# Seven-product gate tiles: the rest of a pair behind the next tile's first copy, the fourth weight sum ahead of the row scaling, an own place for the second gate tile

## The reference, cut to what matters

```python
def swiglu(h, wg, wu, wd):            # h 512x1024, wg and wu 1024x2816, wd 2816x1024
    return (jax.nn.silu(h @ wg) * (h @ wu)) @ wd

for i in range(2):
    x = x + 0.5 * swiglu(rmsnorm_2(x, ffn_norm1[i]), ffn1_wg[i], ffn1_wu[i], ffn1_wd[i])
    # ... attention ...
    x = x + 0.5 * swiglu(rmsnorm_2(x, ffn_norm2[i]), ffn2_wg[i], ffn2_wu[i], ffn2_wd[i])
```

## Time and profile before

| | |
|---|---|
| median of 3 runs | 2733.34 us (2733.22 to 2733.67) |
| profiled execution | 2736.7 us, its span 2735.5 us |
| PE busy | 2645.6 us, 97% of the span |
| DVE, ACT, POOL busy | 1572.2, 1084.5, 598.2 us |
| mean granted clock of TensorE | 0.987 |

### The profile page before, as it was taken

One profiled execution on the slowest core, in us unless ns is written; L12 is line 12 of the kernel. 1 busy time (PEld: TensorE's weight loads), 2 busy tenths in 40 slices (PEclk: granted clock), 3 DMA queues, 4 the chain that ended last, 5 costly groups with the idle time before them and its releaser, 6 DMA issues.

```text
span 2735.5 us, 33395 instructions
## 1 busy us (share of the span) xinstructions
PE 2645.6 (97%) x13532; PEld 2254.5 (82%) x13532; DVE 1572.2 (57%) x2410; ACT 1084.5 (40%) x1797; POOL 598.2 (22%) x574
## 2 busy tenths in 40 slices
PE   9999999999999999999989999999999999899998
PEld 8888888888887887889878888788888888788887
DVE  7538457574766444457774545664545685654543
ACT  4344234242553222257642323442324685432322
POOL 0000010000120000036521312323222685322220
PEclk9999999999999999999999999999999999999999
DMA  5322325323323444364223232232322101232322
GB/s 157 124 93 80 106 95 186 131 78 109 106 77 108 108 90 108 81 121 118 79 70 107 78 108 93 77 116 81 108 81 92 36 32 47 77 108 69 117 62 78
DMA packets 276401, 259.07 MB, mean 95 GB/s; under 512 B 40324, under 2 KB 266647, under 8 KB 276247
## 3 DMA queue, kind: packets, MB, share of 16 engines
q1 hardware_dynamic: 276231, 256.93, 31.2%
q10 hardware_dynamic: 16, 0.00, 0.0%
HBM read 242.23 MB, written 14.68 MB: 94 GB/s over the span
## 4 chain that ended last, share of the span: by engine, by line
PE 70%; issue 9%; DVE 7%; POOL 7%; ACT 4%; DMA 3%; POOLq 0%; SPq 0%; ACTq 0%; DVEq 0%
PE bank L1464 21%; PE bank L1466 21%; PE bank L1465 21%; DMA RAW<-in_ffn_wg 3%; PE bank L1564 1%; PE bank L1565 1%; PE bank L1566 1%; POOL M L2887 1%; POOL TMP L2908 1%; POOL M L2885 1%; POOL RAW L2895 1%; DVE Wl L2267 1%; POOL RAW L2888 1%; PE bank L1651 1%; DVE bank L2374 1%
## 5 line engine op out<-in xcount | busy, mean ns | idle before, releaser
L1464 PE MATMUL bank<-Hh,Wl 128*128 128x512 f32 x1704 | 674.7, 396 | 17.7 <-DVE Wl L2267 16.9
L1465 PE MATMUL bank<-Hl,Wh 128*128 128x512 f32 x1704 | 667.0, 391 | 0.0
L1466 PE MATMUL bank<-Hh,Wh 128*128 128x512 f32 x1704 | 666.5, 391 | 0.0
L2267 DVE TENSOR_TENSOR Wl<-RAW,Wh 128x1024 fp32r<-128x1024 f32 (+1 forms) x366 | 473.1, 1335 | 138.2 <-ACT Wh L1864 137.6
L1864 ACT ACTIVATE Wh<-RAW 128x1024 fp32r<-128x1024 f32 (+2 forms) x400 | 387.3, 1019 | 271.1 <-PE bank L1466 213.9
L1464 PE MATMUL bank<-Ph,Wl 128*128 128x512 f32 x1152 | 451.9, 392 | 0.8 <-DVE Wl L2267 0.4
L1466 PE MATMUL bank<-Ph,Wh 128*128 128x512 f32 x1152 | 448.6, 389 | 0.0
L1465 PE MATMUL bank<-Pl,Wh 128*128 128x512 f32 x1152 | 448.1, 389 | 0.0
L1464 PEld LDWEIGHTS bank<-Hh,Wl 128*128 128x128 f32 x1704 | 322.2, 189 | 87.8 <-DVE Wl L2267 19.2
L1466 PEld LDWEIGHTS bank<-Hh,Wh 128*128 128x128 f32 x1704 | 321.7, 189 | 68.5
L1465 PEld LDWEIGHTS bank<-Hl,Wh 128*128 128x128 f32 x1704 | 322.3, 189 | 65.7 <-issue 1.7
(11 more groups left out here) (385 smaller groups left out, 4073.8 us busy)
## 6 DMA issues: line engine op xcount, KB each, us to landing
RAW<-in_ffn_wg SPq DMA_DIRECT2D x44, 1024.0 KB, 5.3
RAW<-in_ffn_wu SPq DMA_DIRECT2D x44, 1024.0 KB, 5.4
RAW<-in_ffn_wd SPq DMA_DIRECT2D x32, 1024.0 KB, 4.9
RAW<-in_w_up SPq DMA_DIRECT2D x22, 1024.0 KB, 5.1
RAW<-in_w_in SPq DMA_DIRECT2D x20, 1024.0 KB, 5.2
RAW<-in_ffn_wd SPq DMA_DIRECT2D x16, 768.0 KB, 4.2
bias_scratch<-M SPq DMA_DIRECT2D x16, 512.0 KB, 7.9
RAW<-in_w_down SPq DMA_DIRECT2D x8, 1024.0 KB, 5.0
```

Of the source, the lines that this page charges most:

```text
L1464: mm(o, ll, rh, start=start, stop=False)
L1465: mm(o, lh, rl, start=False, stop=False)
L1466: return mm(o, lh, rh, start=False, stop=stop)
L2267: tt(wflat(Wl, o + x, o + y), RAW[:, n % 2, x:y], f(wflat(Wh, o + x, o + y)), ALU.subtract).then_inc(*w_lo.up(*([("w_lo", n)] if i else [])))
```

## The change

Four things change in the list of steps and one in `places`.

- In `pair_seven`, what remains of a pair's second channel group (scaling of the second b bank, multiply, high and low half) is no longer issued at the pair's end. It is kept in `tails` and issued in the next pair, behind copy 1 and ahead of c11 and of the split of the b tile; at the end of a third it is issued at once. c11 now comes ahead of the split.
- The fourth weight sum becomes a piece of its own, 4, and is issued between fill 0 and fill 1, so ahead of the row scalings in POOL's queue.
- `pair_eight` is written anew: in (0,0) the two following tiles are split early (`plain`), both b banks are made in one go, and four `combine` steps stand at the end; in (0,1) eight `combine` steps are dealt out and fills 1, 0, fourth sum, 2, 3 follow. Its second channel group also goes to `tails`.
- `extra(4)` is no longer called ahead of pairs, only ahead of d tiles.
- In `places`, the second dense gate tile, (0,1), goes to the region ends, not to mid.

```diff
--- before.py
+++ after.py
@@ -222,7 +222,7 @@
                 pieces = [(2048 * ends + 1024 * side, 1024), (2048 * mid, 1024), (2048 * mid + 1024, 1024)]
                 side = 1 - side
             else:
-                region = mid if x == "a" else other if x == "b" else (ends, mid, other, ends)[key[1]]
+                region = (ends if key[1] else mid) if x == "a" else other if x == "b" else (ends, mid, other, ends)[key[1]]
                 pieces = [(2048 * region, 2048)]
             if x == "d" and key[1] == 3:
                 if key[0] < 2:
@@ -278,8 +278,9 @@
             if piece == "sums":
                 do("w_sum", n)
                 continue
-            if piece == 3:
+            if piece == 4:
                 do("w_sum4", n)
+                continue
             do("w_fill", n, piece)
             if piece == 3:
                 assert now["split"] == n
@@ -472,7 +473,7 @@
         do("mark", ("up", tag))
         gname, gbase = GAINS[tag]
         keys = hkeys()
-        combos = []
+        combos, tails = [], []
         for r in range(4):
             combos.append(lambda r=r: do("hc_raw", tag, r, xv[2 * r:2 * r + 2], gname, gbase))
             combos.append(lambda r=r: do("hc_sum", tag, r))
@@ -488,6 +489,17 @@
             if i in (1, 2, 5):
                 banks.take((PRODUCTS[i][3], n))
             do("prod", n, i, tag, keys)
+
+        def tail():
+            while tails:
+                tails.pop(0)()
+
+        def finish(h, j, c):
+            b, t = (tag + "b", h, j, c), ("t_a", tag, h, j, c)
+            if c:
+                scale([b])
+            do("glu", t, b)
+            pair_p(2 * j + c, "tmp", t, ("glu", t))
 
         def pair_seven(h, j, last_pair):
             n = next_tile(tag + "a", (h, j), 0)
@@ -498,8 +510,9 @@
             for c in range(2):
                 tmps.take(t[c])
             do("cp", n, 1, t)
+            tail()
+            do("c11", n, t)
             plain(n + 1)
-            do("c11", n, t)
             norm_step()
             prod(n, 6)
             do("cp", n, 2, t)
@@ -513,7 +526,7 @@
             if last_pair:
                 plain(n + 2)
             else:
-                feed(n + 2, 0, 1)
+                feed(n + 2, 0, 4, 1)
             dense([bb[0]], nb, 8, "H")
             scale([bb[0]])
             prod(n, 4)
@@ -530,67 +543,59 @@
                 feed(n + 2, 2, 3)
             for m in range(2):
                 do("silu_f", n, m, t)
-            for m in range(2):
-                if m:
-                    scale([bb[1]])
-                do("glu", t[m], bb[m])
-                pair_p(2 * j + m, "tmp", t[m], ("glu", t[m]))
+            finish(h, j, 0)
+            tails.append(lambda: finish(h, j, 1))
 
         def pair_eight(h, j):
-            begins = (h, j) == (0, 0)
+            begins = j == 0
             ba, bb = ([(tag + x, h, j, c) for c in range(2)] for x in "ab")
-            na = next_tile(tag + "a", (h, j), 1)
+            na = next_tile(tag + "a", (h, j), 1 if begins else 0)
+            if not begins:
+                feed(na + 2, "sums")
             dense(ba, na, 8, "H", scaled=not begins, wide=begins)
             do("used", na)
             if begins:
                 norm_step()
-                combine(2)
-                nb = next_tile(tag + "b", (h, j), 1)
-                feed(na + 2, "sums")
-                dense(bb[0:1], nb, 8, "H")
-                combine(2)
-                dense(bb[1:2], nb, 8, "H", kw=1)
+                plain(na + 2)
+                nb = next_tile(tag + "b", (h, j), 0)
+                dense(bb, nb, 8, "H")
                 do("used", nb)
                 scale(ba)
-                feed(na + 2, 0)
+                for c in range(2):
+                    do("silu", ba[c], tmps.take(("t_a", tag, h, j, c)))
+                plain(nb + 2)
+                scale(bb[0:1])
+                finish(h, j, 0)
+                finish(h, j, 1)
+                combine(4)
+                return
             for c in range(2):
-                t = tmps.take(("t_a", tag, h, j, c))
-                do("silu", ba[c], t)
-            if begins:
-                combine(2)
-                feed(na + 2, 1, 2, 3)
-                scale(bb)
-            else:
-                nb = next_tile(tag + "b", (h, j), 1)
-                feed(na + 2, "sums", 0)
-                combine(3)
-                dense(bb[0:1], nb, 8, "H")
-                scale(bb[0:1])
-                feed(na + 2, 1)
-                combine(2)
-                dense(bb[1:2], nb, 8, "H", kw=1)
-                do("used", nb)
-                feed(na + 2, 2, 3)
-                scale(bb[1:2])
-            for c in range(2):
-                t = ("t_a", tag, h, j, c)
-                do("glu", t, bb[c])
-                pair_p(2 * j + c, "tmp", t, ("glu", t))
-            if begins:
-                combine(2)
+                do("silu", ba[c], tmps.take(("t_a", tag, h, j, c)))
+            feed(na + 2, 1)
+            combine(3)
+            nb = next_tile(tag + "b", (h, j), 0)
+            dense(bb[0:1], nb, 8, "H")
+            scale(bb[0:1])
+            finish(h, j, 0)
+            feed(na + 2, 0, 4)
+            combine(3)
+            dense(bb[1:2], nb, 8, "H", kw=1)
+            do("used", nb)
+            feed(na + 2, 2, 3)
+            combine(2)
+            tails.append(lambda: finish(h, j, 1))
 
         for h, (c0, n) in enumerate(THIRDS):
             last = (tag, h) == ("s3", 2)
             if last:
                 todo[:] = [lambda i=i: x_turn(i // 4, i % 4) for i in range(8)]
             for j in range(n // 2):
-                if (h, j) != (0, 0):
-                    extra(4)
                 if (h, j) >= FIRST_SEVEN:
                     assert not combos
                     pair_seven(h, j, j == n // 2 - 1)
                 else:
                     pair_eight(h, j)
+            tail()
             if h == 2:
                 h_new(tag + "_after")
                 do("mark", ("mfree", tag))
@@ -606,7 +611,7 @@
                 if h < 2 and i == 2:
                     feed(nd + 2, "sums", 1, 2)
                 if h < 2 and i == 3:
-                    feed(nd + 1, 0, 3)
+                    feed(nd + 1, 0, 4, 3)
                 for c in range(2):
                     add_x(2 * i + c, bd[c], 0.5)
                     if h == 2:
```

## The result

| | before | changed |
|---|---|---|
| median of 6 runs each, same chip | 2733.51 us (2732.80 to 2734.62) | 2686.95 us (2684.99 to 2689.51) |
| profiled execution, its span | 2736.7, 2735.5 us | 2684.99, 2683.5 us |
| PE busy, share of the span | 2645.6 us, 97% | 2625.1 us, 98% |
| mean granted clock | 0.987 | 0.995 |

The ratio is 0.983, with a 95% interval of 0.9817 to 0.9843: 46.6 us gained, where 42.1 were forecast. The two profiled spans differ by 51.9 us, of which 2.35 us lie ahead of stage s1, where nothing was changed; that part is scatter between executions.

What follows compares the result with a forecast made beforehand. The matmul row is busy for 97% of the span, so only TensorE's waits and slow stretches can be won. Steady pairs and s3's last third gain 48.7 us, openings lose 6.6: 42.1 gained, median 2691.2 us (2681 to 2702).

Steps and rivals of the forecast that it cites:

- step 1: Steady pair: fourth sum ends by about 12.5 us, before the scalings; fill 3 follows fill 2 at once, silus earlier.
- step 2: Steady pair: with the rest behind copy 1, product 6's 2.31 us wait goes, with 0.8 us to spare.
- steps 3 and 4: Steady pairs with sums: VectorE's low halves, alone in time, meet POOL's sums; b half at 8.13 against 7.19, waiting 0.94 us.
- the condition that the prediction gave for no wait: Pairs with sums: if the low half wins the race for the port against POOL's sum, no wait.
- The sum of the steady pairs: Sixteen pairs: 18.5 us without sums, 11.0 with sums, 12.5 from the clock; last third of s3 6.7; together 48.7 gained.
- The eight falls of the clock: After 8 of 16 waits at product 6 the clock falls, 1.57 us each; all go, 12.5 us gained.
- The openings: Stage openings: s1 1.9 us gained, s2 2.9 and s3 4.0 lost; with 1.6 for a clock fall, 6.6 us lost.
- The same walk from the end of s3's first b tile: Opening of s3: s2's walk shifted 599.9 us later puts the b half at 2402.4 against 2398.39, 4.0 us lost.
- Rival A: Low half wins the port in most pairs, openings come out even: 56 us gained, 2677; A or better, chance 0.20.
- B: Port takes 1.9 us in 8 pairs, some clock falls stay, openings lose 15: 2711; or worse but faster, chance 0.23.
- C: POOL's queue: fourth sum waits for a late low half 0, delaying scalings, silus and copy 1; slower, e.g. 2745; chance 0.03.
- D: Product 6 is released by the high combinations or low half 1, not copy 1; nothing gained, 2733; chance 0.02.

Runs made afterwards that it cites:

- Experiment 2: Kernel before with only the fourth weight sum moved between fills 0 and 1, ahead of the row scalings: 2689.01 us, ratio 0.9832.
- experiment 5: Changed kernel with the old opening (`pair_eight`, `extra` and `places` as before): 2684.66 us, ratio 0.9817.
- experiment 6: Changed kernel with the rounds of combined inputs dealt out early again in the opening, early splits kept: 2670.05 us, ratio 0.9763.
- experiment 7: Changed kernel with the turned copy issued behind the silus and channel 0 in the last third of s3: 2678.22 us, ratio 0.9794.
- Experiment 4: Changed kernel with POOL's three weight sums of the next seven-product tile waiting for the b tile's low halves: 2676.40 us, ratio 0.9786.
- experiment 1: Kernel before with only the rest of a pair's second channel group put behind copy 1, c11 ahead of the split: 2705.56 us, ratio 0.9893.
- experiment 8: Changed kernel with mixed opening, weight sums behind the b tile's low halves and late turned copy, all together: 2654.67 us, ratio 0.9708.

## Why the prediction was right, step by step

**The fourth sum early (step 1): right, and the larger cause than the prediction makes it.** ScalarE's wait for L2900 is gone from steady pairs, the load is issued 1.98 us ahead of product 1 (1.92 predicted). Experiment 2 shows that this alone releases product 6. The prediction told of it as what brings the silus and channel 0 forward, and gave the removal of the wait to step 2; the wait has two removers, and outside the openings and the last third of s3 each alone suffices: 29.6 us for step 2 alone, 46.1 us for step 1 alone, 46.6 us for both with the new opening, 50.2 us for both without it (experiment 5). Step 2 is the weaker because it leaves the fourth sum late, so that b tile's split, behind copy 1 and the rest, comes 1.4 to 2.1 us late (b offsets 8.57 and 9.26 instead of 7.19).

**Product 6 (step 2): right.** Start +2.87, walked 2.88.

**The port (steps 3 and 4): right, and decided by which of the two starts first.** Sum start +3.43 (walked 3.44), low half +3.52 (3.61), b half +8.10 (8.13; the prediction's own 3.44 + 4.67 is 8.11). The wait came in six of the eight pairs with sums, 0.86 us each on average; in (2,1) of s2 and (1,1) of s3 it did not. The order in time tells why. In the six pairs the sum starts 0.08 to 0.20 us ahead of the low half. In the other two it starts 0.01 and 0.02 us behind it, and then the sum is the one that takes longer. This is pair (2,1) of s2, VectorE and POOL:

```profile
2014.24 3.46 DVE L2272 TENSOR_TENSOR Wl<-RAW,Wh 128x1024 fp32r<-128x1024 f32 x2
...
2014.25 2.36 POOL L2890 TENSOR_TENSOR M<-RAW 128x512 f32<-128x512 f32 x1 [4.94 <-DMA RAW<-in_ffn_wg]
```

That is the condition that the prediction gave for no wait. In experiments 2, 5, 6 and 7 the sum started first in all eight pairs, and the wait came in all eight, 0.6 to 0.9 us. Experiment 4 shows that the cause is the meeting of the two engines: with the sums moved, the same low halves take half the time and the wait is gone everywhere. The Trainium skill (SBUF — State Buffer, section Who interferes with whom) says that the pair of ports is an exclusive lock and that issue order decides who blocks; the trace agrees, in the six pairs and in the two.

**The sum of the steady pairs.** Predicted 42.0 us for the sixteen (18.5 + 11.0 + 12.5) and 6.7 for the last third of s3. Measured 44.3 and 6.4, and 0.3 us elsewhere. Of the 2.3 us too little, 1.9 are the two waits of 0.94 that did not come, and 0.5 that the six others are 0.86. The eight falls of the clock are gone: the granted clock is 1.00 over the three long stretches above, and its mean rose from 0.987 to 0.995.

**The openings: sign and size right for s1 and s2, too dark for s3.** Product 1 of the next pair: s1 2.2 gained (1.9 walked), s2 2.6 lost (2.9), s3 1.0 lost where 4.0 were walked. And the 1.6 us for one more fall of the clock did not appear, though the clock did fall (0.73 on average over the window above). Net 1.4 lost, not 6.6. Two terms were too large:

- "The same walk from the end of s3's first b tile": the walk shifted the whole chain by the 5.5 us by which the norm's result R comes later in s3's opening than in s2's. But in s2 the chain is not led by R. Order in time, ScalarE, the high halves of the second b tile, in s2 and in s3 of the changed kernel (with what stands ahead of them in s3):

```profile
1743.61 2.01 ACT L1869 ACTIVATE Wh<-RAW 128x1024 fp32r<-128x1024 f32 x2 [2.98 <-PE bank L1471]
...
2326.79 1.09 ACT L2024 ACTIVATE TMP<-bank 128x512 f32<-128x512 f32 x2
2327.76 2.01 ACT L1869 ACTIVATE Wh<-RAW 128x1024 fp32r<-128x1024 f32 x2
```

 In s2 the split stands 2.98 us waiting for PE to leave the region of the first b tile; in s3 it does not wait. From the stage's first product they are at 23.87 and 26.65, 2.78 apart, and everything behind keeps that distance: b half at 62.08 and 64.85. R's lateness first fills s2's wait, and only the rest shifts the chain. This was not tried apart; it is read from the two openings of one kernel.
- The clock: in the opening of s2 it is at the lower of its two levels behind the wait at product 6, and products 6 and 5 take 5.9 us, 0.4 of it waiting, where 2.9 would do. But product 7 behind them waits for copy 2 (0.40 us) and the b half for the low halves of its tile (0.52 us, above), and neither of these waits for the slow products. So the products fill a wait that would else be longer, and the fall cost nothing there.

**The median.** The profiled gain is 9.8 us above the 42.1 of the forecast: 5.2 from the openings, 2.3 from the pairs and the last third, 2.3 ahead of s1. The medians show only 4.5 us more, since the profiled run before stood 3.2 us above its median of 2733.51 and the one after 2.0 us below its own: the forecast misses 2686.95 by 4.3 us. Rival A (2677) foresaw openings that come out even and a port that is never met: the first nearly came, the second did not. B is refuted by its three terms: six port waits of 0.86 us, no fall in a steady pair, 1.4 us lost in the openings. C's POOL queue did not come about: in all 27 pairs the first row scaling (L2913) waits for VectorE's addition L2306, so the fourth sum ahead of it in the queue was done in time. D is refuted by product 6.

## What to carry to other kernels

When an engine waits, look at what stands ahead of its releaser in the releaser's in-order queue, and go on from queue to queue: here TensorE's 2.3 us came from a copy on ScalarE behind a silu behind a sum on GpSimd behind a row scaling, and moving the sum ahead of the two row scalings gave 46.1 of the 50.2 us that both edits give together (experiments 2 and 5). The gains of two edits that each open the same queue do not add up (29.6 and 46.1 us alone, 50.2 together), so try each alone before paying for both. And where two engines that slow each other start within 0.2 us, order them by a wait on purpose: it cost TensorE nothing here and gave 8.3 us by the profiled spans, 10.5 by the medians.

## What the runs showed that was not expected

- The split delay of experiment 1 cost no clock. Single waits of 2.15 us were followed by a lower granted clock at 8 of 16 places in the kernel before; in experiment 1 the pairs with sums still lose 2.07 us each, in two waits of 1.17 and 0.52 us by the records, and no pair shows a fall; the mean clock is 0.994. Not every split did so: in the last third of s3 of the changed kernel a wait of 1.81 us at product 6 (2600.92) was followed by a fall (granted 0.58 from 2602 to 2606 us), though only 0.49 us more was waited at the next one.
- Starting 0.01 us ahead of POOL's sum or 0.09 us behind it is the difference between 3.46 us and no wait and 4.53 us and a wait of 0.75 us, in pairs of one execution; apart from the sums the same two low halves take 2.36 us. The scatter from run to run cannot be put down to this: experiments 5 and 6, which have the meeting, spread over 1.4 and 1.3 us, like experiment 8 (1.3), which has not; the changed kernel's six runs spread over 4.5 us, and why stays open.
